# Two GpSimd steps and a later sum in the first pass of a retention stage

## The chip, the cores and the metric

The kernel runs on one core of one Trainium2 chip. The metric is the device time of one execution in microseconds (us), less is better. A measurement is a set of executions; the median is compared.

## What is computed

The kernel runs a two-layer backbone over 256 context tokens and 1024 latent tokens of width 1024. In each layer one combined projection feeds four mixers (a short convolution, latent attention, RWKV-7 and retention); their outputs are joined and projected, and a mixture of 16 experts follows. The change lies in retention alone, whose start is:

```python
def rotate(t, cos, sin):
    t1, t2 = jnp.split(t, 2, axis=-1)
    return jnp.concatenate([t1 * cos - t2 * sin, t1 * sin + t2 * cos], axis=-1)

def ret_project(z, rot):
    q, k, v, g = jnp.split(z.astype(jnp.float32), 4, axis=-1)
    q = split_heads(q, RET_HEADS) * (RET_DK ** -0.5)
    k = split_heads(k, RET_HEADS)
    if rot is not None:
        q = rotate(q, *rot)
        k = rotate(k, *rot)
    return q, k, split_heads(v, RET_HEADS), g

# per chunk of 128 tokens, for each of 4 heads (64 wide), forward and on flipped tokens:
    zeta = jnp.exp((RET_CHUNK - 1 - j)[:, None] * log_gamma[None, :])
    d_r = jnp.einsum('bnchk,bnchv->bnhkv', kc * zeta[None, None, :, :, None], vc)
    r_state * dec_c + dr_i
```

Context tokens are not rotated (`rot` is None), latent tokens are.

## The kernel before

Each layer runs as a row of stages. Each stage is one or more blocks, in which every engine has its own list of instructions and waits on semaphores; all engines meet at the end of a block. `stage_retention` has two blocks. The first one, here called the first pass, walks over the 10 tiles of 128 tokens (tiles 0 and 1 are context, 2 to 9 latent) in order. The change touches only this pass, once in each layer.

What each engine's list holds for tile t in the first pass, with the lines of the profile:

- **SyncE** (`rows_in`, L1353 and L1355) loads the tile's projected row `z` (128x1024, 512 KB) and, for latent tiles, the table `rope` (64 KB) into one of two slots. From tile 2 on it waits until the sum of tile t-2 is written and V of tile t-2 is copied.
- **VectorE** (`rotated`) makes the 8 heads of queries and keys, `qk`: for a context tile one copy (L1390); for a latent tile the direct product `ra` = z times cosine (L1393, 128x512), the crossed product `rb` = the other half of z times sine (L1396, two instructions of 8 runs of 32 columns), and their sum (L1398). Then `scaled_queries` (L1406, `QX`, two instructions) and `forward_state` (L1413, `SF`, two instructions, reading the forward sums from PSUM).
- **TensorE** (`turned`, L1471) transposes the tile's `qk` in four instructions; `sums` (L1484) makes keys times values of the tile before, 16 small products (8 of each direction) from `kz` and `V`.
- **ScalarE** computes the gate and copies V (`gate_values`, L1431 and L1432; here G and V), weighs the keys for the two directions (`weighed_keys`, L1450, 8 instructions of 128x64), copies the transposes out of PSUM (`turned_out`, L1436, `QT`) and copies the backward sums (`backward_sum`, L1440).
- **GpSimd** has nothing in this block. It makes the backward states (L1599, L1601) in the second one.

The order in these lists is written out by hand. VectorE's loop was: the rotation of tile t+1, then `QX` of tile t, then `SF` of tile t-1. ScalarE's loop: G and V of tile t+1, `kz` of t, `QT` of t, backward sum of t-1. TensorE's: transposes of t, sums of t-1.

The buffers that join the engines are `z`, `rope`, `qk` and `kz`, two slots each, and `ra` and `rb`, one each.

## Time and profile before

| what | us |
|---|---|
| median of 3 executions | 4108.26 |
| lowest, highest | 4102.06, 4124.47 |
| the profiled execution's own time | 4104.09 |
| span of its trace | 4102.3 |
| the first pass in layer 0, from 720.4 to 762.7 | 42.3 |
| the first pass in layer 1, from 2848.3 to 2890.2 | 41.9 |

Over the whole span TensorE is busy for 89%, VectorE for 54%, ScalarE for 26% and GpSimd for 12%. The shares are averages over stages that differ: the two first passes together are 84.2 us, 2.1% of the span, and have to be read by themselves, from the timeline. In them a row of the timeline gives the start, the length, the engine, the line, the tile written and the tiles read, how many instructions are merged in the row, and in brackets how long the engine was idle before it and who released it. Merged instructions overlap a little, so two of 0.42 can show as 0.76.

### The profile page before, as it was taken

To read this page: it belongs to the slowest core of one execution; us is meant where nothing else is said; L and a number is where in the kernel's file an instruction comes from. 1 tells how busy PE (TensorE), PEld (TensorE's weight loads), DVE (VectorE), ACT (ScalarE), POOL (GpSimd) and SP (SyncE) were. 2 spreads that over 40 slices of the span, in tenths; PEclk is the share of its full clock that TensorE was granted. 3 is DMA by queue.
4 is the path that set the end of the run, shared out by engine and by line. 5 is a ranking of instruction groups with operands and counts; after the bars stand their busy time and mean duration, and the time that the engine had idled before them with its cause. 6 is when DMAs were issued, how large, how long until landed. Compare 5 with 4: busy or idle time off the path is not lost. (4 is left out here: it accounts for less than half of the span.)

```text
span 4102.3 us, 65871 instructions
## 1 busy us (share of the span) xinstructions
PE 3640.6 (89%) x27258; PEld 2016.9 (49%) x27258; DVE 2226.3 (54%) x3698; ACT 1063.0 (26%) x2366; POOL 490.1 (12%) x675
## 2 busy tenths in 40 slices
PE   7899999687896699999997899998697876999998
PEld 4555665476633233333333655674586532333333
DVE  2554324687745644444443554335778667655654
ACT  3442110634311111111111542112544211212121
POOL 1100000231201011111111200000232110010100
PEclk9999999698998799999998999998698987999999
DMA  6200120200275587777774100121100336999996
GB/s 252 104 1 11 58 76 0 90 4 19 74 259 219 209 272 262 261 261 261 261 254 138 34 6 11 59 70 47 43 10 13 120 130 237 341 320 332 326 323 209
DMA packets 293591, 613.12 MB, mean 149 GB/s; under 512 B 37640, under 2 KB 50184, under 8 KB 286640
## 3 DMA queue, kind: packets, MB, share of 16 engines
q1 hardware_dynamic: 272752, 542.32, 37.2%
q0 software_dynamic: 20544, 66.60, 6.3%
q8 instruction: 219, 3.59, 0.4%
q14 instruction: 76, 0.62, 0.0%
HBM read 561.07 MB, written 47.79 MB: 148 GB/s over the span
## 5 line engine op out<-in xcount | busy, mean ns | idle before, releaser
L2991 PE MATMUL ps<-moe_w,e_hT 128*128 128x512 f32 x1024 | 449.4, 597 | 21.2 <-issue 9.2
L3120 DVE TENSOR_TENSOR moe_w<-moe_w 128x2048 f32<-128x2048 f32 x128 | 287.2, 2286 | 206.1 <-PE ps L2922 160.5
L2892 PE MATMUL ps<-moe_w,e_xs 128*64 128x512 f32 x1536 | 348.6, 596 | 0.8 <-DVE moe_w L3120 0.8
L2892 PE MATMUL ps<-moe_w,e_xT 128*64 128x512 f32 x1536 | 345.8, 600 | 0.8 <-DVE moe_w L3120 0.8
L2991 PEld LDWEIGHTS ps<-moe_w,e_hT 128*128 128x128 f32 x1024 | 192.3, 190 | 258.1 <-issue 255.3
L3126 DVE TENSOR_TENSOR e_cb<-e_part,ps 128x512 f32<-128x512 f32 x128 | 87.8, 686 | 335.1 <-ACT e_part L3028 249.2
L2892 PEld LDWEIGHTS ps<-moe_w,e_xT 128*64 128x64 f32 x1536 | 111.9, 139 | 222.9 <-issue 222.8
L2892 PEld LDWEIGHTS ps<-moe_w,e_xs 128*64 128x64 f32 x1536 | 105.4, 137 | 193.7 <-issue 192.3
L1184 PE MATMUL ps<-M 96*128 96x512 f32 (+1 forms) x400 | 182.4, 542 | 3.7 <-PEq L749 2.1
L3028 ACT COPY e_part<-ps 128x512 f32<-128x512 f32 x96 | 56.2, 585 | 487.4 <-PE ps L2892 479.1
L478 ACT COPY yT<-ps 128x256 f32<-128x256 f32 (+1 forms) x90 | 42.4, 471 | 402.8 <-PE ps L390 402.8
L1048 PE MATMUL ps<-yT,hT 128*128 128x272 f32 (+1 forms) x608 | 145.5, 393 | 0.0
L3120 DVE TENSOR_TENSOR moe_w<-e_t,moe_w 128x2048 f32<-128x2048 f32 x64 | 143.5, 2284 | 0.0
L1196 PEld LDWEIGHTS ps<-all_tabs,a_pr 128*128 128x128 f32 x656 | 74.6, 142 | 129.8 <-issue 88.3
L3120 DVE TENSOR_TENSOR e_t<-moe_w 128x2048 f32<-128x2048 f32 x60 | 134.6, 2284 | 0.0
L1245 DVE COPY a_pt<-ps 128x512 f32<-128x512 f32 (+1 forms) x104 | 61.2, 589 | 129.1 <-PE ps L1196 128.5
L1196 PE MATMUL ps<-all_tabs,a_pr 128*128 128x128 f32 x656 | 111.9, 284 | 20.4 <-ACT a_pt L1245 13.8
L2854 POOL DMA_INDIRECT x_rows<-e_ye,all_tok x16 | 52.7, 3291 | 639.4 <-DVE e_ye L3161 639.4
L1260 DVE TENSOR_REDUCE a_mx<-ps 128x1 f32<-128x1280 f32 (+1 forms) x72 | 98.5, 1368 | 52.0 <-PE ps L1184 52.0
L1048 PEld LDWEIGHTS ps<-yT,hT 128*128 128x128 f32 x608 | 113.6, 195 | 21.5 <-issue 1.3
L2854 POOL DMA_INDIRECT out_dram<-e_ye,all_tok x16 | 52.2, 3263 | 598.5 <-DVE e_ye L3161 598.5
L1287 ACT ACTIVATE a_pr<-ps,a_mx 128x1280 f32<-128x1280 f32 (+1 forms) x72 | 88.7, 1232 | 112.7 <-DVE a_mx L1261 112.7
(417 smaller groups left out, 7075.4 us busy)
## 6 DMA issues: line engine op xcount, KB each, us to landing
moe_w<-in_w_gate_dram SPq DMA_DIRECT2D x128, 1024.0 KB, 13.7
moe_w<-in_w_up_dram SPq DMA_DIRECT2D x128, 1024.0 KB, 14.2
moe_w<-in_w_down_dram SPq DMA_DIRECT2D x128, 1024.0 KB, 12.9
m_mod_w<-in_w_ada_dram SPq DMA_DIRECT2D x24, 1024.0 KB, 6.6
o_mod_w<-in_w_ada_dram SPq DMA_DIRECT2D x24, 1024.0 KB, 7.6
yT<-in_w_in_dram SPq DMA_DIRECT2D x6, 2048.0 KB, 8.6
r_z<-z_rows SPq DMA_DIRECT2D x20, 512.0 KB, 3.3
z_rows<-p_zo POOLq DMA_DIRECT2D x36, 256.0 KB, 2.3
```

The costliest lines, as they stand in the source:

```text
L1048: ins = nc.tensor.matmul(ps[:, ZBANK[a], 0:hi - lo], hT[:, k, t * P:(t + 1) * P], w[:, k, lo:hi], start=(k == 0), stop=(k == KT - 1))
L1184: ins = nc.tensor.matmul(ps[:, SB[u % 2] + i, 0:w], QT[0:QK, h, t * P:(t + 1) * P], KTr[0:QK, h, n:n + w], start=True, stop=True)
L1196: ins = nc.tensor.transpose(ps[:, TB, k * P:(k + 1) * P], pr[:, u % NP, (k0 + k) * P:(k0 + k + 1) * P], g.ident)
L1245: copy(pt[:, k % 2, u % 2, k0:k0 + nk].rearrange("p k n -> p (k n)"), ps[:, TB, 0:nk * P]).then_inc(*done.up())
L1260: link(nc.vector.reduce_max(mx[:, s % 2, 0:1], src, AX_X))
L1287: nc.scalar.activation(pr[:, s % NP, 0:units[s][2] * P], src, ACT.Exp, bias=mx[:, s % 2, 1:2], scale=SCALE, accum_out=rs[:, s // 2 % 4, s ...
L2854: pool.indirect_dma_start(dst, bass.IndirectOffsetOnAxis(ap=g.tok[:, 0, e:e + 1], axis=0), ye[:], None, compute_op=ALU.add).then_inc(*sc.u ...
L2892: ins = nc.tensor.matmul(ps[HF * q:HF * q + HF, b, :], x[:, k], weights[q][:, k], start=(first and k == 0), stop=(k == 3), skip_group_chec ...
L2991: ins = nc.tensor.matmul(ps[:, YB + c, :], hT2[:, 4 * half + k], quarter(name, e)[:, k], start=(half == 0 and k == 0), stop=(half == 1 and ...
L3028: nc.scalar.copy(part[:, i], ps[:, A_]).then_inc(*tcd.up())
L3120: nc.vector.tensor_tensor(to, a, b, ALU.subtract).then_inc(*td.up())
L3126: nc.vector.tensor_tensor(out_of(c), part[:, 1 if c == C12 else 0], ps[:, b], ALU.subtract if c == C21 else ALU.add).then_inc(*cd.up())
```

## The change

1. VectorE no longer makes the crossed product. GpSimd does, with the same two instructions of 8 runs of 32 columns (`crossed_part`), for latent tiles.
2. The keys weighed for the backward direction, four ScalarE instructions of 128x64 before, become one GpSimd instruction of 128x256 (`weighed_backward`). ScalarE keeps the four of the forward direction.
3. The rotation is split: the direct product of tile t+1 (`direct_part`) stays at the head of VectorE's loop, the sum (`rotated`) moves behind `QX` of tile t and `SF` of tile t-1.
4. New semaphores: `rad` (direct product), `rbd` (crossed product), `kzb` (backward keys). VectorE's sum waits for all three, TensorE's `sums` for `kzb`.

```diff
--- before.py
+++ after.py
@@ -1343,6 +1343,7 @@
         z_in, small, chain = [sg(f"w_slot{i}") for i in range(2)], sg("small_in"), sg("dve_chain")
         qkd, tr, ev_a, vd = sg("normed"), sg("transposed"), sg("evac_a"), sg("rt_zd")
         kzd, rm, fw, bw, wiped = sg("rt_kz"), sg("rt_rm"), sg("rt_rev"), sg("rt_bw"), sg("coef")
+        rad, rbd, kzb = sg("rt_ra"), sg("rt_rb"), sg("rt_kzb")
         with nc.Block() as block:
             @block.sync
             def _(sp):
@@ -1373,28 +1374,31 @@
                     n += 16 if u < NCT else 32
                 return n
 
+            def z8(t):
+                return z[:, t % 2, 0:512].rearrange("p (h d) -> p h d", h=8)
+
             @block.vector
             def _(dve):
                 link = linker(dve, chain)
 
+                def direct_part(t):
+                    dve.wait_ge(*z_in[t % 2].at(z_at(t)))
+                    if t >= NCT:
+                        if t > NCT:
+                            dve.wait_ge(*qkd.at(t))
+                        nc.vector.tensor_tensor(ra[:], z8(t), rope[:, t % 2, 0].unsqueeze(1).broadcast_to([P, 8, HD]), ALU.mult).then_inc(*rad.up())
+
                 def rotated(t):
-                    zz, q = z[:, t % 2], qk[:, t % 2]
-                    dve.wait_ge(*z_in[t % 2].at(z_at(t)))
-                    z8 = zz[:, 0:512].rearrange("p (h d) -> p h d", h=8)
-                    if t >= 1:
-                        dve.wait_ge(*qkd.at(t))
+                    q = qk[:, t % 2]
                     if t >= 2:
                         dve.wait_ge(*tr.at(t - 1))
                         dve.wait_ge(*kzd.at(t - 1))
+                        dve.wait_ge(*kzb.at(t - 1))
                     if t < NCT:
-                        nc.vector.tensor_copy(q, z8).then_inc(*qkd.up())
+                        nc.vector.tensor_copy(q, z8(t)).then_inc(*qkd.up())
                     else:
-                        r = rope[:, t % 2]
-                        link(nc.vector.tensor_tensor(ra[:], z8, r[:, 0].unsqueeze(1).broadcast_to([P, 8, HD]), ALU.mult))
-                        for s in range(2):
-                            a, b = 32 * s, 32 * (1 - s)
-                            link(nc.vector.tensor_tensor(rb[:, :, a:a + 32], z8[:, :, b:b + 32],
-                                                         r[:, 1, a:a + 32].unsqueeze(1).broadcast_to([P, 8, 32]), ALU.mult))
+                        dve.wait_ge(*rad.at(t - NCT + 1))
+                        dve.wait_ge(*rbd.at(t - NCT + 1))
                         nc.vector.tensor_tensor(q, ra[:], rb[:], ALU.add).then_inc(*qkd.up())
 
                 def scaled_queries(t):
@@ -1416,13 +1420,43 @@
 
                 link(nc.vector.memset(SF[:, 0], 0.0))
                 nc.vector.memset(ps[:, 2:6], 0.0).then_inc(*wiped.up())
+                direct_part(0)
                 rotated(0)
                 for t in range(NT):
                     if t + 1 < NT:
-                        rotated(t + 1)
+                        direct_part(t + 1)
+                    if t == 0:
+                        rotated(1)
                     scaled_queries(t)
                     if t >= 1:
                         forward_state(t - 1)
+                    if 1 <= t < NT - 1:
+                        rotated(t + 1)
+
+            @block.gpsimd
+            def _(pool):
+                def crossed_part(t):
+                    pool.wait_ge(*z_in[t % 2].at(z_at(t)))
+                    if t > NCT:
+                        pool.wait_ge(*qkd.at(t))
+                    for i in range(2):
+                        a, b = 32 * i, 32 * (1 - i)
+                        ins = nc.gpsimd.tensor_tensor(rb[:, :, a:a + 32], z8(t)[:, :, b:b + 32],
+                                                      rope[:, t % 2, 1, a:a + 32].unsqueeze(1).broadcast_to([P, 8, 32]), ALU.mult)
+                    ins.then_inc(*rbd.up())
+
+                def weighed_backward(t):
+                    if t == 0:
+                        pool.wait_ge(*small.at(80))
+                    pool.wait_ge(*qkd.at(t + 1))
+                    if t >= 2:
+                        pool.wait_ge(*rm.at(t - 1))
+                    nc.gpsimd.tensor_tensor(kz[:, t % 2, 1], qk[:, t % 2, 4:8].rearrange("p h d -> p (h d)"), ze[:, 1], ALU.mult).then_inc(*kzb.up())
+
+                for t in range(NT):
+                    if NCT <= t + 1 < NT:
+                        crossed_part(t + 1)
+                    weighed_backward(t)
 
             @block.scalar
             def _(act):
@@ -1445,10 +1479,9 @@
                     act.wait_ge(*qkd.at(t + 1))
                     if t >= 2:
                         act.wait_ge(*rm.at(t - 1))
-                    for d in range(2):
-                        for h in range(H):
-                            ins = nc.scalar.activation(kz[:, t % 2, d, h * HD:(h + 1) * HD], qk[:, t % 2, 4 + h], ACT.Copy,
-                                                       scale=ze[:, d, h * HD:h * HD + 1])
+                    for h in range(H):
+                        ins = nc.scalar.activation(kz[:, t % 2, 0, h * HD:(h + 1) * HD], qk[:, t % 2, 4 + h], ACT.Copy,
+                                                   scale=ze[:, 0, h * HD:h * HD + 1])
                     ins.then_inc(*kzd.up())
 
                 gate_values(0)
@@ -1474,6 +1507,7 @@
 
                 def sums(t):
                     pe.wait_ge(*kzd.at(t + 1))
+                    pe.wait_ge(*kzb.at(t + 1))
                     pe.wait_ge(*vd.at(t + 1))
                     if t >= 2:
                         pe.wait_ge(*fw.at(t - 1))
```

VectorE before, first pass of layer 0, from the rotation of tile 2 on. The rows give line, operation, tile written, tiles read and shape; x2 means two in a row:

```order
L1393 TENSOR_TENSOR r_ra<-r_z,r_rope 128x512
L1396 TENSOR_TENSOR r_rb<-r_z,r_rope 128x8x32 x2
L1398 TENSOR_TENSOR r_qk<-r_ra,r_rb 128x512
L1406 TENSOR_TENSOR r_QX<-r_QT,r_xi 128x2x128 x2
L1413 SCALAR_TENSOR_TENSOR r_SF<-r_SF,r_gd,ps 128x128 x2
```

VectorE in the changed kernel, the same place:

```order
L1389 TENSOR_TENSOR r_ra<-r_z,r_rope 128x512
L1410 TENSOR_TENSOR r_QX<-r_QT,r_xi 128x2x128 x2
L1417 SCALAR_TENSOR_TENSOR r_SF<-r_SF,r_gd,ps 128x128 x2
L1402 TENSOR_TENSOR r_qk<-r_ra,r_rb 128x512
L1389 TENSOR_TENSOR r_ra<-r_z,r_rope 128x512
```

The crossed product is gone from the list, and the sum (L1398 before, L1402 now) stands behind `QX` and `SF`.

GpSimd in the changed kernel, first pass of layer 0, from its start; before there was no row of this engine here:

```order
L1454 TENSOR_TENSOR r_kz<-r_qk,r_ze 128x256
L1444 TENSOR_TENSOR r_rb<-r_z,r_rope 128x8x32 x2
L1454 TENSOR_TENSOR r_kz<-r_qk,r_ze 128x256
L1444 TENSOR_TENSOR r_rb<-r_z,r_rope 128x8x32 x2
L1454 TENSOR_TENSOR r_kz<-r_qk,r_ze 128x256
```

The crossed product of tile t+1 stands ahead of the backward keys of tile t, all the way to the end of the pass.

## Rows read from the trace of the kernel before

**Rows 1.** The page's first line: span and number of instructions.

```profile
span 4102.3 us, 65871 instructions
```

**Rows 2.** Stretches: length; busy PE, PEld, DVE, ACT, POOL; clock; DMA share; GB/s.

```profile
720.40:762.70 42.30, 21.67 (x200) 16.51 (x200) 31.88 (x74) 34.90 (x121) 0.00 (x0) 0.50 0.47 156
...
733.55:758.63 25.08, 15.17 (x140) 11.55 (x140) 23.62 (x58) 23.49 (x86) 0.00 (x0) 0.50 0.45 142
2861.54:2886.13 24.59, 15.20 (x140) 11.58 (x140) 23.51 (x58) 23.47 (x85) 0.00 (x0) 0.50 0.45 145
```

**Rows 3.** Timeline, layer 0: the sum of tile 2 to the sum of tile 5.

```profile
732.86 0.69 DVE L1398 TENSOR_TENSOR r_qk<-r_ra,r_rb 128x512 f32<-128x512 f32 x1
...
733.58 0.33 SPq L1353 DMA_DIRECT2D r_z<-z_rows  x1
...
733.61 1.12 PE L1471 MATMUL ps<-all_tabs,r_qk 128*128 128x128 f32 x4 [2.46 <-DVE r_qk L1398]
...
738.08 0.42 ACT L1431 ACTIVATE r_G<-r_z 128x256 f32<-128x256 f32 x1 [0.96 <-DMA r_rope<-const_rope_r_dram]
...
738.24 1.12 PE L1484 MATMUL ps<-r_V,r_kz 128*64 128x64 f32 x16
...
738.70 2.02 ACT L1450 ACTIVATE r_kz<-r_qk,r_ze 128x64 f32<-128x64 f32 x8
...
740.62 0.56 ACT L1436 COPY r_QT<-ps 128x512 f32<-128x512 f32 x1
...
741.22 0.76 DVE L1406 TENSOR_TENSOR r_QX<-r_QT,r_xi 128x256 f32<-128x256 f32 x2 [0.64 <-ACT r_QT L1436]
...
741.89 0.60 DVE L1413 SCALAR_TENSOR_TENSOR r_SF<-r_SF,r_gd,ps 128x128 f32<-128x128 f32 x2
...
742.41 0.69 DVE L1393 TENSOR_TENSOR r_ra<-r_z,r_rope 128x512 f32<-128x512 f32 x1
743.13 0.88 DVE L1396 TENSOR_TENSOR r_rb<-r_z,r_rope 128x256 f32<-128x256 f32 x2
...
744.05 0.69 DVE L1398 TENSOR_TENSOR r_qk<-r_ra,r_rb 128x512 f32<-128x512 f32 x1
```

**Rows 4.** Timeline, layer 0: load of tile 7 issued, and its first reader.

```profile
744.77 0.33 SPq L1353 DMA_DIRECT2D r_z<-z_rows  x1
...
748.43 0.42 ACT L1431 ACTIVATE r_G<-r_z 128x256 f32<-128x256 f32 x1 [0.44 <-DMA r_rope<-const_rope_r_dram]
```

**Rows 5.** Timeline, layer 1: load of tile 4 issued, and its first reader.

```profile
2861.57 0.33 SPq L1353 DMA_DIRECT2D r_z<-z_rows  x1
...
2865.65 0.42 ACT L1431 ACTIVATE r_G<-r_z 128x256 f32<-128x256 f32 x1 [0.67 <-DMA r_rope<-const_rope_r_dram]
```

**Rows 6.** Timeline, layer 0: first keys weighed, and the end of the pass.

```profile
727.96 2.02 ACT L1450 ACTIVATE r_kz<-r_qk,r_ze 128x64 f32<-128x64 f32 x8 [1.91 <-DMA r_gr<-in_g_ret_norm_dram]
...
757.94 0.69 DVE L1398 TENSOR_TENSOR r_qk<-r_ra,r_rb 128x512 f32<-128x512 f32 x1
...
761.86 0.60 DVE L1413 SCALAR_TENSOR_TENSOR r_SF<-r_SF,r_gd,ps 128x128 f32<-128x128 f32 x2
761.90 0.37 ACT L1440 COPY yT<-ps 128x256 f32<-128x256 f32 x1 [0.48 <-PE ps L1484]
```

**Rows 7.** GpSimd and VectorE lines of the second block: ns min/median/max, first and last start.

```profile
L1599 POOL TENSOR_TENSOR r_SB<-r_SB,r_gd x18: 602/612/614, 763.1 to 2909.1; 128x256 f32<-128x256 f32 x18
...
L1601 POOL TENSOR_TENSOR r_SB<-r_SB,yT x18: 717/834/843, 763.8 to 2909.7; 128x256 f32<-128x256 f32 x18
...
L1578 DVE TENSOR_TENSOR r_on<-r_on,r_G x18: 424/424/427, 770.8 to 2920.4; 128x256 f32<-128x256 f32 x18
```

**Rows 8.** Timeline, second block: GpSimd beside a VectorE instruction with two SBUF inputs.

```profile
770.83 0.42 DVE L1578 TENSOR_TENSOR r_on<-r_on,r_G 128x256 f32<-128x256 f32 x1
771.00 0.84 POOL L1601 TENSOR_TENSOR r_SB<-r_SB,yT 128x256 f32<-128x256 f32 x1
```

## Prediction

> **What bounds the kernel now.** I read the timeline of the two first passes, since the page's shares say nothing about 2% of a span of 4102.3 us [rows 1]. Let S(t) be the end of the sum of tile t. Seven periods lie between S(2) = 732.86 + 0.69 = 733.55 and S(9) = 757.94 + 0.69 = 758.63 [rows 3, 6]: 25.08 us in layer 0, and 24.59 in layer 1, so 3.58 and 3.51 us a tile. VectorE is busy for 23.62 of the 25.08 and ScalarE for 23.49, GpSimd for nothing [rows 2]. The reader should see two nearly full engines and conclude, first, that taking work from both ought to help; and then look at what fills a period. VectorE's list goes `ra`, `rb`, sum, `QX`, `SF`, by starts 742.41, 743.13, 744.05 and 741.22, 741.89 [rows 3]: from `QX` to `SF` 0.67, from `SF` to `ra` 0.52, `ra` 0.72, `rb` 0.92, sum 0.69, together about 3.5. This order has a property that no busy share shows. Behind S(t) VectorE had 2.3 us of rotation of the next tile to do while TensorE transposed and ScalarE copied out, so `QX` seldom waited.
>
> A second chain runs through the loads. `z` and `rope` have two slots, so tile t+2 is asked for at S(t): 733.58 for tile 4, behind S(2) = 733.55. ScalarE's G of tile 4 starts at 738.08, released by the `rope` load [rows 3]. I call this L = time from S(t) to G of tile t+2: 4.53 there, 4.11 for the same tile in layer 1 (2865.65 less 2861.54) [rows 2, 5], 3.69 for tile 7 (748.43 less the end of the sum at 744.05 + 0.69 = 744.74) [rows 3, 4]. G stands ahead of `kz` and `QT` of the tile before in ScalarE's list. So S(5) = S(2) + L 4.53 + G and V 0.62 + eight `kz` 1.92 + `QT` to `QX` 0.60 + 0.67 + 0.52 + the rotation 2.33 = 744.74, which is just the 744.05 + 0.69 of the trace [rows 3]. Before, this chain spanned three tiles, 11.19 at worst, and bit once a layer.
>
> **The change part by part.** *Crossed product off VectorE.* Two instructions, 0.92 us of a period [rows 3], are taken from VectorE. *Backward keys off ScalarE.* Four of eight instructions at 1.92 / 8 = 0.24 each by starts: 0.96 [rows 3]. As engine work this leaves VectorE 2.6 and ScalarE about 2.3 us a tile. *The sum moved last.* Here the gain goes. The sum of tile t+1 now stands behind `QX` of tile t, which waits for `QT` of t, which waits for the transposes of t, which wait for S(t). Of the rotation only `ra` (0.69) still lies under that latency. From S(t) on: 0.06 to the first transpose (733.61 less 733.55), 1.12 for the four, 0.04 to ScalarE, so `QT` starts at +1.22; the four `kz` of about 0.05 + 0.96 = +1.01 are just hidden beside them. Then `QT` start to `QX` start 0.60, `QX` to `SF` 0.67, `SF` to what follows 0.52, sum 0.69 [rows 3]. That is **3.70 us** from S(t) to S(t+1), against 3.58 and 3.51 before. TensorE's 16 products of `sums` follow the transposes by 1.04 or so and take 1.12 [rows 3], ending at +2.3, ahead of `SF` at +2.49: hidden.
>
> *GpSimd's side.* Its three instructions are released at S(t) too. The trace has no product of 8 runs of 32 columns on this engine. The nearest rows are its 128x256 products and sums, 0.61 and 0.72 to 0.84 [rows 7]; a short run could be up to twice as dear. A pair at 0.61 to 0.84 takes 1.2 to 1.7; even if it starts only behind `ra`, at +0.72, it is there by +1.9 to +2.4, and the sum starts at +3.01. It is covered, and stays so up to 1.14 us an instruction. The backward keys, one more of 0.6 to 0.84, end by +3.3 and are asked for by `sums` in the next period, at about +1.1 there: covered.
>
> *The two engines at once.* With both on the same SBUF tiles they may hold each other up. Where `r_on<-r_on,r_G` of VectorE (both inputs in SBUF) overlapped GpSimd's L1601, GpSimd took 0.84 in place of 0.72, while VectorE kept its 424 ns, at most 427 over 18 [rows 7, 8]. No row that I read shows a VectorE instruction of this kind that starts in the middle of a GpSimd one. The bounds are 0 and a full block of `QX` until GpSimd is done (the rival below, 1.1 us a tile); I take c = 0.15 a tile, near the row, since `QX` at +1.82 meets at most the end of the second crossed instruction. The period is 3.85.
>
> *The loads' chain gets shorter in tiles.* Now S(t+2) = S(t) + L + 0.62 + 0.96 + 0.60 + 0.67 + 0.52 + 0.69 = S(t) + L + 4.06 + c: it spans two tiles where it spanned three. With L = 3.69 that is 7.90 for two tiles, 3.95 each, a little over 3.85; with the slow first loads it is 8.74 in layer 0 and 8.32 in layer 1. Nothing hides this.
>
> *Start and end of the pass.* `kz` of tile 0 starts at 727.96 when the constants have landed [rows 6]. Then `QT` +0.96, G and V of tile 2 +0.60, `kz` of 1 +0.62, `QT` +0.96, `QX` +0.60, `SF` +0.67, sum +0.52, its end +0.69: S(2) = 733.58, as before (733.55): what the four `kz` give is paid for by the sum's place. Behind S(9) the last copy ended at 761.90 + 0.37 = 762.27, 3.64 later, and `SF` at 762.46, 3.83 later [rows 6]. Now the sums of tile 9 end at about +3.2 and their copy at +3.6, and `SF` at +3.1: 0.2 gained.
>
> *The sum.* With these rules, layer 0: S(2) 733.7, S(3) 737.6, S(4) 742.5 (loads), S(5) 746.3, S(6) 750.4, S(7) 754.2, S(8) 758.3, S(9) 762.1, against 758.63: +3.5. Layer 1: +3.6. Less 0.2 each: +6.7 us in all. Engines meet at the block's end, so the shift passes to the end of the kernel whole, and nothing behind it changes. Against the profiled execution's own time, 4104.09 + 6.7 = 4110.8; I say **4111**. That execution lay 4.2 below the median of its three (4108.26), so a median might well read 4115. With c = 0 it is +5.2.
>
> **The rivals.**
>
> *A, the engines' work decides (faster).* If `QT` came much sooner than I reckon, the period would be VectorE's 2.6, held by the loads to at least (3.69 + 4.06) / 2 = 3.88 unless G's wait too were gone. At 2.6 a tile, seven periods give 18.2, about 6.6 less a layer, 4091. Against it: the trace shows every link of the 3.70, and none is GpSimd's or `rb`.
>
> *B, the loads are quick (no difference).* If L falls to 3.3 or less, the period is 3.70 all through: 25.9 a layer, +0.8 and +1.3, less 0.4: 4106. For it: L varies from 4.53 to 3.69. Against: each L measured is over 3.6.
>
> *C, the engines shut each other out (slower).* `QX`'s two instructions start at +1.82, when GpSimd is in its run of three. If GpSimd, once it has begun, is let through to its end (0.72 + 3 times 0.73 = +2.9), `QX` comes 1.1 late in each period: 4.8 a tile, S(9) at 768.4 in layer 0, +9.7 and +10.1, less 0.4, 4123.5; if VectorE slips in ahead of the backward keys, c = 0.8 and 4119. It decides from the point where GpSimd still holds the tiles at +1.82, that is, once a crossed instruction takes over 0.55 us behind `ra`. For it: the 0.12 that GpSimd lost beside VectorE [rows 8]. Against: VectorE itself has lost nothing in 18 instances [rows 7]. The Trainium skill, "SBUF — State Buffer", section "Who interferes with whom", says that a VectorE instruction with two SBUF inputs contends with a GpSimd instruction that reads SBUF, and that whoever starts first gets the shared pair for the whole instruction. By that rule `ra`, `QX` and the sum all contend, and the outcome is this rival's 4119 to 4123.5 in place of 4111; the 0.12 us of the row agrees with its half in which GpSimd is the loser.
>
> **How the numbers follow.** Forecast (c from 0 to 0.3: 4109 to 4112.5) 0.60; C (4117 to 4124) 0.20; B 0.10; A 0.06; something in GpSimd that is dearer than twice its rows, beyond 4124, 0.04. Eight in ten, with the few us by which medians of this kernel stand from the profiled execution, need 4100 to 4123. About 0.5%, 20 us, is what a measurement of this kernel can tell from no change (its three times spread over 22). Nearly all cases lie inside: faster by more 0.03, within 0.92, slower by more 0.05.
>
> **What would show it.** In the changed trace: `QX` idle in each period, released by `QT`; the time from transposes to `QT` start to `QX` to `SF` to sum of 3.7 to 3.85; in every other period ScalarE's G released by `rope` with `kz` right behind it; VectorE's busy time down by about 6 of 23.6 us in this stretch and its idle time up by more; `rb` on GpSimd done before `SF` starts. C is told by `QX` starting well after `QT`'s end, or by `QX` or GpSimd rows longer than 0.42 and 0.84. I am wrong if the sum waits for GpSimd, if the gap S(2) to S(9) shrinks below 25, or if the time moves outside the two first passes.

## The result, and the profile after

The changed kernel takes 4124.11 us (median of 20 executions, 4109.93 to 4137.73) against 4109.41 us before (median of 20, 4098.97 to 4124.47): the ratio is 1.004, with a 95% interval from 1.0029 to 1.0051. It is slower by 14.7 us, inside the half per cent called no change ahead of the result. The forecast was 4111 with a range from 4100 to 4123, so it missed, its upper end by 1.1 us. The profiled execution of the changed kernel took 4124.27 us.

The page's first line and the stretches of the changed kernel, as [rows 1, 2] show them of before. The columns of a stretch are its length, then busy PE, PEld, DVE, ACT and POOL, then the clock, the DMA share and GB/s; DVE is VectorE, ACT ScalarE, POOL GpSimd, PE TensorE, PEld its weight loads, and further down SPq the queue of SyncE. The first two stretches are the first passes of layers 0 and 1, the third runs from S(2) to S(9) of layer 0, where S(t) is the end of the sum of tile t as in the prediction:

```profile
span 4122.1 us, 65855 instructions
...
720.22:769.98 49.76, 21.52 (x200) 16.42 (x200) 29.88 (x58) 27.70 (x81) 23.36 (x27) 0.50 0.40 133
2847.61:2897.21 49.60, 21.53 (x200) 16.44 (x200) 29.86 (x58) 27.29 (x81) 23.34 (x27) 0.50 0.41 133
735.18:766.22 31.04, 15.17 (x140) 11.55 (x140) 22.07 (x43) 18.04 (x54) 19.31 (x21) 0.50 0.35 115
```

Two things are to be seen. The passes are 49.8 and 49.6 us long. And VectorE is still busy for 22.07 us between S(2) and S(9), where it was for 23.62 [rows 2]: 14 crossed instructions are gone from that stretch, with 0.88 x 7 = 6.2 us of busy time [rows 3], but the busy time fell by only 1.55. What is left of its list has grown by some 4.6 us.

To compare kernels I take a pass from the first issue of a `z` load to GpSimd's first memset of the second block. By that measure both passes together are 84.16 us before (42.27 and 41.89) and 99.36 after (49.76 and 49.60), so 15.2 us more, against 14.7 in the medians. Where they sit:

| part of the pass | layer 0 before, after | layer 1 before, after | difference | forecast |
|---|---|---|---|---|
| first load issued to S(2) | 13.07, 14.96 | 13.19, 14.48 | +1.89, +1.29 | about 0 |
| seven periods, S(2) to S(9) | 25.08, 31.04 | 24.59, 31.36 | +5.96, +6.77 | +3.5, +3.6 |
| S(9) to the end | 4.12, 3.76 | 4.11, 3.76 | -0.36, -0.35 | -0.2, -0.2 |
| sum | | | +15.2 | +6.7 |

One period of the changed kernel, timeline of layer 0 from S(2) = 735.18 to S(3) = 739.51. The columns are start, length, engine, line, operation, tile written and tiles read, number of merged instructions, and the idle time before with its releaser:

```profile
735.24 1.11 PE L1504 MATMUL ps<-all_tabs,r_qk 128*128 128x128 f32 x4 [5.00 <-DVE r_qk L1402]
...
735.28 0.69 DVE L1389 TENSOR_TENSOR r_ra<-r_z,r_rope 128x512 f32<-128x512 f32 x1
735.33 1.93 POOL L1444 TENSOR_TENSOR r_rb<-r_z,r_rope 128x256 f32<-128x256 f32 x2 [1.88 <-DVE r_qk L1402]
...
736.39 0.59 ACT L1470 COPY r_QT<-ps 128x512 f32<-128x512 f32 x1
737.00 1.39 DVE L1410 TENSOR_TENSOR r_QX<-r_QT,r_xi 128x256 f32<-128x256 f32 x2 [1.03 <-ACT r_QT L1470]
737.21 0.91 POOL L1454 TENSOR_TENSOR r_kz<-r_qk,r_ze 128x256 f32<-128x256 f32 x1
...
738.32 0.59 DVE L1417 SCALAR_TENSOR_TENSOR r_SF<-r_SF,r_gd,ps 128x128 f32<-128x128 f32 x2
...
738.83 0.68 DVE L1402 TENSOR_TENSOR r_qk<-r_ra,r_rb 128x512 f32<-128x512 f32 x1
```

The first half is the forecast's, to within 0.01 us: `QT` starts at S + 1.21 (forecast 1.22), `QX` at S + 1.82 (forecast 1.82), and `QX` has waited 1.03 us for `QT`. From there on it is not. `QX` takes 1.39 us where it took 0.76 [rows 3], and `SF` starts 1.32 behind it, not 0.67. The period is 1.21 + 0.61 + 1.32 + 0.51 + 0.68 = 4.33 us, and 4.32 to 4.33 in six of the seven of each layer.

The same lines over both passes, ns min/median/max of one instruction, then first and last start:

```profile
L1410 DVE TENSOR_TENSOR r_QX<-r_QT,r_xi x40: 412/521/943, 729.6 to 2895.6; 128x256 f32<-128x256 f32 x40
...
L1444 POOL TENSOR_TENSOR r_rb<-r_z,r_rope x32: 716/978/1240, 730.9 to 2890.5; 128x256 f32<-128x256 f32 x32
...
L1454 POOL TENSOR_TENSOR r_kz<-r_qk,r_ze x20: 720/900/913, 728.0 to 2893.5; 128x256 f32<-128x256 f32 x20
```

A `QX` instruction took 418 to 427 ns before. Now half of them take over 521, up to 943. GpSimd's instructions take 716 and 720 at best and up to 1240. The trace even holds its own control, at the end of layer 0's pass, where there is no further tile to rotate and GpSimd makes the backward keys alone, well ahead of `QX`:

```profile
766.29 0.73 POOL L1454 TENSOR_TENSOR r_kz<-r_qk,r_ze 128x256 f32<-128x256 f32 x1 [1.48 <-DVE r_qk L1402]
...
768.04 0.76 DVE L1410 TENSOR_TENSOR r_QX<-r_QT,r_xi 128x256 f32<-128x256 f32 x2 [1.82 <-ACT r_QT L1470]
```

Both engines are back to 0.73 and 0.76. It looks like the third rival, the engines shutting each other out. Whether it is that, and how much of the loss it makes, the experiments tell.

### The profile page after: what moved, and what is told of

Same layout as the page of the kernel before. It is cut to its first block and busy times, and to the rows that moved or that the text cites. A ratio compares the mean times of both kernels' runs of the same rounds, so it can differ in the third digit from the quotient of the medians.

```text
span 4122.1 us, 65855 instructions
## 1 busy us (share of the span) xinstructions
PE 3640.0 (88%) x27258; PEld 2018.0 (49%) x27258; DVE 2222.4 (54%) x3666; ACT 1049.2 (25%) x2286; POOL 537.6 (13%) x727
## 6 DMA issues: line engine op xcount, KB each, us to landing
moe_w<-in_w_gate_dram SPq DMA_DIRECT2D x128, 1024.0 KB, 14.1
```

## The experiments

The theories. **Contention**: the 0.63 us a tile is VectorE and GpSimd holding each other up when both read SBUF. **Order**: whatever the contention, the sum's place costs by itself. **Loads**: the passes are held up by the two slots. The table gives what each run showed; a pass is measured as above, periods are S to S, and a time is a median where there are several executions, with its ratio to the kernel before as it was measured beside that run.

| run | both passes, us | typical period | time, us |
|---|---|---|---|
| before | 84.16 | 3.43 to 3.47 | 4109.41 (20) |
| after | 99.36 | 4.33 | 4124.11 (20), 1.004 |
| e1_write_only | 91.08 | 3.69 to 3.72 in six of 14, others to 4.24, one 4.82 | 4110.73 (1) |
| e2_no_backward | 92.67 | 3.80 to 4.01, one 5.55 | 4115.14 (1) |
| e3_cross_vector | 92.99 | 3.81 to 4.12, three 4.56 to 5.43 | 4116.09 (1) |
| e4_sum_first | 86.58 | 3.46 and 3.62, one 4.92 | 4107.63 (10), 1.0003 |
| e5_third_slot | 99.28 | 4.33 | 4122.07 (1) |
| e6_queries_psum | 85.24 | 3.48 | 4112.13 (1) |
| e7_all_three | 78.19 | 3.03 | 4100.34 (12), 0.9974 |
| e8_before_third_slot | 86.99 | 3.43 | 4110.06 (10), 0.9998 |
| e9_order_alone | 104.77 | 4.50 | 4132.06 (1) |
| e10_first_psum | 84.34 | 3.24 and 3.64 | 4114.83 (1) |
| e11_all_three_late | 77.07 | 3.03 | 4102.94 (12), 0.9988 |

A single time says little here. The span less the two passes, which no edit touches, lies between 4015.6 and 4029.4 us in these traces: 14 us of spread that belong to none of the changes. What follows is read from the passes, and times decide only where there are ten or more. The passes have a spread of their own: from the first load issued to the first keys, which wait for the small constants, it is 7.3 to 7.9 us in most traces with two slots, but 9.21 and 8.13 in e4_sum_first, 8.27 and 8.78 in e9_order_alone and 8.10 in layer 0 of e10_first_psum, though SyncE's list is the same in all of them. The periods don't contain this part and are the surer measure.

### GpSimd writes only

```diff
-                        nc.vector.tensor_tensor(q, ra[:], rb[:], ALU.add).then_inc(*qkd.up())
+                        nc.vector.tensor_tensor(q, ra[:], ra[:], ALU.add).then_inc(*qkd.up())
...
-                    for i in range(2):
-                        a, b = 32 * i, 32 * (1 - i)
-                        ins = nc.gpsimd.tensor_tensor(rb[:, :, a:a + 32], z8(t)[:, :, b:b + 32], ..., ALU.mult)
-                    ins.then_inc(*rbd.up())
+                    scratch = SB[:].rearrange("p t a n -> p (t a n)")
...
+                    nc.gpsimd.memset(scratch[:, 0:1856], 0.0).then_inc(*rbd.up())
...
+                        nc.gpsimd.memset(SB[:].rearrange("p t a n -> p (t a n)")[:, 1856:2560], 0.0).then_inc(*kzb.up())
```

> The changed kernel, but GpSimd only writes: its two crossed products are one memset of 1856 columns of an unused buffer (estimated 1.7 us from the 1.38 us of its 1536-column memset in the trace of before), and its backward keys of tiles 2 to 9 a memset of 704 columns (0.7 us); the sum on VectorE adds the direct product to itself. That leaves out the crossed half of the rotation and the backward keys. GpSimd stays busy for as long as before, at the same places. Theory 1 (VectorE's instructions with two SBUF inputs and GpSimd's reads shut each other out): QX's two take 0.76 us again in place of 1.39, and the period of a tile is 1.21 + 0.61 + 0.67 + 0.51 + 0.68 = 3.7 us, up to 3.9 where the loads hold it, in place of 4.33. Theory 2 (any work of GpSimd beside VectorE slows it, writes too): QX stays at 1.2 us or more and the period at 4.2 or more.

The same period in layer 0, timeline, and the line of `QX` over both passes:

```profile
735.15 1.65 POOL L1445 MEMSET r_SB<- 128x1856 f32 x1 [1.84 <-DVE r_qk L1402]
...
736.73 0.68 POOL L1457 MEMSET r_SB<- 128x704 f32 x1
...
736.87 0.76 DVE L1410 TENSOR_TENSOR r_QX<-r_QT,r_xi 128x256 f32<-128x256 f32 x2 [1.03 <-ACT r_QT L1473]
...
L1410 DVE TENSOR_TENSOR r_QX<-r_QT,r_xi x40: 411/422/460, 729.9 to 2892.0; 128x256 f32<-128x256 f32 x40
```

GpSimd is busy beside all of `QX` but its last 0.22 us (to 737.41 of 737.63), and `QX` takes its 0.76. The period is 3.70 where no load is late: the forecast's sum with c = 0, c being its term for what the two engines take from each other. So it is not GpSimd's being busy, nor its writing to SBUF, that stretches `QX`; it is its reading. The Trainium skill, "SBUF — State Buffer", section "Who interferes with whom", says that a VectorE instruction with two SBUF inputs contends with a GpSimd instruction that reads SBUF and not with one that only writes it; these rows agree on the half about writing, and the `QX` of 1.39 in the changed kernel on the half about reading.

### No backward keys on GpSimd

```diff
-                    nc.gpsimd.tensor_tensor(kz[:, t % 2, 1], qk[:, t % 2, 4:8].rearrange("p h d -> p (h d)"), ze[:, 1], ALU.mult).then_inc(*kzb.up())
+                    if t < 2:
+                        nc.gpsimd.tensor_tensor(kz[:, t % 2, 1], qk[:, t % 2, 4:8].rearrange("p h d -> p (h d)"), ze[:, 1], ALU.mult).then_inc(*kzb.up())
+                    else:
...
+                        nc.gpsimd.memset(SB[:, 0, 0, 0:1], 0.0).then_inc(*kzb.up())
```

> The changed kernel, but GpSimd's backward keys of tiles 2 to 9 are left out (a memset of one column signals in their place). Theory 1: QX's first instruction keeps its 0.53 us (it meets the end of the crossed product), the second falls from 0.94 to 0.42, since nothing reads beside it; the period falls by 0.52 to 3.8 us, 3.9 where the loads hold it. Theory 2, or if the second crossed instruction alone is the obstacle: the period stays over 4.2.

`QX` in layer 0, timeline: the pair, and in an answer that starts later its first instruction alone:

```profile
737.70 0.86 DVE L1410 TENSOR_TENSOR r_QX<-r_QT,r_xi 128x256 f32<-128x256 f32 x2 [1.03 <-ACT r_QT L1474]
```
```profile
737.70 0.53 DVE L1410 TENSOR_TENSOR r_QX<-r_QT,r_xi 128x256 f32<-128x256 f32 x1 [1.03 <-ACT r_QT L1474]
```

The first instruction still takes 0.53 (it meets the end of the crossed product, as in the changed kernel), the second is free, and the period is 3.81 where no load is late. That splits the 0.63 of the changed kernel: 0.11 come from the crossed product, 0.52 from the backward keys, which start between the two `QX` instructions and shut the second one out.

### The crossed product back on VectorE

```diff
                         nc.vector.tensor_tensor(ra[:], z8(t), rope[:, t % 2, 0].unsqueeze(1).broadcast_to([P, 8, HD]), ALU.mult).then_inc(*rad.up())
+                        for i in range(2):
+                            a, b = 32 * i, 32 * (1 - i)
+                            ins = nc.vector.tensor_tensor(rb[:, :, a:a + 32], z8(t)[:, :, b:b + 32], ..., ALU.mult)
+                        ins.then_inc(*rbd.up())
...
                 for t in range(NT):
-                    if NCT <= t + 1 < NT:
-                        crossed_part(t + 1)
                     weighed_backward(t)
```

> The changed kernel with the crossed product back on VectorE, behind the direct one; the sum stays last and the backward keys stay on GpSimd. This is the order with one GpSimd instruction a tile, which runs beside the products. Theory 1, with the sum's place costing by itself: the products take 1.6 us and up to 0.6 more beside GpSimd's read, so QX starts at 1.82 to 2.2 behind the sum, QX's two take 0.76, and the period is 3.7 to 4.1 us, above the 3.5 to 3.6 of before although GpSimd no longer meets QX. Rival (the sum's place costs nothing, all the loss is contention): 3.5 or less.

Timeline, layer 0:

```profile
734.76 0.74 DVE L1415 TENSOR_TENSOR r_QX<-r_QT,r_xi 128x256 f32<-128x256 f32 x2
...
736.70 0.73 POOL L1459 TENSOR_TENSOR r_kz<-r_qk,r_ze 128x256 f32<-128x256 f32 x1 [3.09 <-DVE r_qk L1407]
...
736.73 1.25 DVE L1389 TENSOR_TENSOR r_ra<-r_z,r_rope 128x512 f32<-128x512 f32 x1
...
738.61 0.76 DVE L1415 TENSOR_TENSOR r_QX<-r_QT,r_xi 128x256 f32<-128x256 f32 x2
```

This shows that either engine can be the one that loses. GpSimd starts 0.03 us ahead and keeps its 0.73; VectorE's `ra` takes 1.25 in place of 0.69, just until GpSimd is done (737.43) and 0.55 more. In the changed kernel `ra` was ahead by 0.05 (735.28, 735.33) and it was GpSimd's first crossed instruction that took 1.24. In these rows whoever begins first keeps its time. And with most of the contention gone from the chain the period is 3.82, still longer than the 3.43 to 3.47 of before. At most 0.13 of that is the stretched `ra`: `QX` of tile 2 starts at S(2) + 1.95 (734.76 less 732.81), where it was + 1.82 in the changed kernel; the rest, over 0.2 us a tile, is not contention.

### The old order, without GpSimd

The kernel before, with only the sum moved behind `QX` and `SF`:

```diff
-                    if t >= 2:
-                        dve.wait_ge(*tr.at(t - 1))
-                        dve.wait_ge(*kzd.at(t - 1))
...
-                        nc.vector.tensor_tensor(q, ra[:], rb[:], ALU.add).then_inc(*qkd.up())
+
+                def summed(t):
+                    if t >= NCT:
+                        dve.wait_ge(*tr.at(t - 1))
+                        dve.wait_ge(*kzd.at(t - 1))
+                        nc.vector.tensor_tensor(qk[:, t % 2], ra[:], rb[:], ALU.add).then_inc(*qkd.up())
...
                         forward_state(t - 1)
+                    if t + 1 < NT:
+                        summed(t + 1)
```

> The kernel before with nothing but the sum moved behind QX and SF; VectorE still makes both products and ScalarE all eight key instructions; GpSimd has no work in the pass, so nothing can contend. Theory (the place of the sum costs the latency through TensorE and ScalarE): behind S(t) the eight key instructions take 0.05 + 1.92 and only then comes QT, so the period is 1.97 + 0.60 + 0.67 + 0.52 + 0.69 = 4.45 us in place of 3.43: the passes get about 14 us longer in all. Rival (the order is harmless by itself): 3.6 or less.

Timeline, layer 0, from S(3) = 739.44:

```profile
739.47 2.02 ACT L1454 ACTIVATE r_kz<-r_qk,r_ze 128x64 f32<-128x64 f32 x8 [1.14 <-DVE r_qk L1400]
...
741.39 0.56 ACT L1440 COPY r_QT<-ps 128x512 f32<-128x512 f32 x1
...
742.06 0.76 DVE L1408 TENSOR_TENSOR r_QX<-r_QT,r_xi 128x256 f32<-128x256 f32 x2 [0.91 <-ACT r_QT L1440]
...
743.25 0.68 DVE L1400 TENSOR_TENSOR r_qk<-r_ra,r_rb 128x512 f32<-128x512 f32 x1
```

No GpSimd, no contention (`QX` 0.76), and the slowest kernel of all: 4.50 a period, both passes 20.6 us longer than before, where about 14 were expected. The seven periods of each layer give 14.8 of it, about as expected; the other 5.8 lie at the start, 1.9 a layer by the new order and 2.0 in all because the constants landed later in this trace. With the sum last, all eight `kz` stand on the chain ahead of `QT`. Moving half of them, and the crossed product, to GpSimd takes the period to 4.33 and the passes from 104.77 to 99.36, 5.4 us less, of which 1.6 are again only the constants. So the order is what makes the changed kernel slower, and the two moves to GpSimd pay back about a fifth of what it costs.

### The new work, with the sum first

```diff
                         direct_part(t + 1)
-                    if t == 0:
-                        rotated(1)
+                        rotated(t + 1)
                     scaled_queries(t)
...
                         forward_state(t - 1)
-                    if 1 <= t < NT - 1:
-                        rotated(t + 1)
```

> The changed kernel with the sum back at its old place, ahead of QX and SF; GpSimd keeps both of its steps. Theory 1: the latency through TensorE and ScalarE is hidden again, so the period is VectorE's work, 0.67 + 0.52 + 0.72 + 0.69 = 2.6 us, and what the two engines take from each other, 0.5 to 1.0, so 3.1 to 3.6 us a tile against 4.33 and against 3.5 of before: 4099 to 4110 us beside a before of 4109. Rival (the order is not to blame, GpSimd's steps are): 4 us a tile or more, 4117 or more.

Timeline, layer 0, and the line of the sum over both passes:

```profile
749.60 2.02 POOL L1441 TENSOR_TENSOR r_rb<-r_z,r_rope 128x256 f32<-128x256 f32 x2 [0.91 <-DMA r_rope<-const_rope_r_dram]
...
751.76 1.10 DVE L1402 TENSOR_TENSOR r_qk<-r_ra,r_rb 128x512 f32<-128x512 f32 x1 [0.71 <-POOL r_rb L1441]
...
752.78 1.28 DVE L1410 TENSOR_TENSOR r_QX<-r_QT,r_xi 128x256 f32<-128x256 f32 x2
...
L1402 DVE TENSOR_TENSOR r_qk<-r_ra,r_rb x16: 691/998/1103, 733.1 to 2886.2; 128x512 f32<-128x512 f32 x16
```

Putting the order back takes 12.8 of the 15.2 us back: 86.58 against 99.36. But the gain of the GpSimd work over the old kernel does not appear (84.16). Of the 2.4 us above it, 1.8 lie before S(2), where the constants came later than before by 1.73 and 0.53; the periods are no shorter either (50.9 in all, 49.7 before). Now the sum waits in every second tile for the crossed product (0.71), whose `rope` landed late, and is itself stretched from 0.69 to a median of 1.00, since the backward keys begin just ahead of it; and `QX` still takes 1.28 in some tiles, beside the crossed product. In time the kernel is the same as before, 1.0003 with an interval from 0.9987 to 1.0019.

### QX from PSUM

`QX` reads the transposes where TensorE left them, and ScalarE's copy of them waits for `QX`. The order stays the changed kernel's.

```diff
-                    dve.wait_ge(*ev_a.at(t + 1))
+                    dve.wait_ge(*tr.at(t + 1))
...
-                        nc.vector.tensor_tensor(QX[:, :, d, ts], QT[:, 0:2, ts], xi[:, :, d], ALU.mult)
+                        ins = nc.vector.tensor_tensor(QX[:, :, d, ts], ps[:, t % 2, 0:2 * P].rearrange("p (a n) -> p a n", a=2), xi[:, :, d], ALU.mult)
+                    ins.then_inc(*qxd.up())
...
-                    act.wait_ge(*tr.at(t + 1))
+                    act.wait_ge(*qxd.at(t + 1))
...
+                        pe.wait_ge(*qxd.at(t - 1))
```

> The changed kernel, but VectorE makes QX straight from the transposes in PSUM, ahead of ScalarE's copy of them, which now waits for QX (one PSUM bank, one engine at a time). Theory: QX starts 1.21 us behind the sum in place of 1.82, and as it has one SBUF input it meets nothing of GpSimd, so its two take 0.76 in place of 1.39. SF then waits for TensorE's sums, at about +2.3, and the sum starts at +2.8: a period of about 3.5 us in place of 4.33, a little more where the loads hold it. If the contention did not come from the second SBUF input, QX would stay at 1.2 us or more: 3.9 or more.

The line of `QX` over both passes, and `SF` in layer 0:

```profile
L1410 DVE TENSOR_TENSOR r_QX<-ps,r_xi x40: 414/417/425, 732.4 to 2889.9; 128x256 f32<-128x256 f32 x40
```
```profile
740.73 0.60 DVE L1418 SCALAR_TENSOR_TENSOR r_SF<-r_SF,r_gd,ps 128x128 f32<-128x128 f32 x2 [0.31 <-PE ps L1520]
```

Of 40 `QX` instructions none is over 425 ns, with GpSimd's list as it was. Having one input in PSUM ends the contention for `QX`; it also takes ScalarE's copy out of the chain. Now `SF` waits for the sums of TensorE, the period is 3.48 and the passes are 14.1 us shorter than the changed kernel's, though the sum still stands last. `QX` from PSUM and the sum first together (e10_first_psum) give little more:

> The version with all three parts less two of them: two load slots again, and the direct product in SBUF, so that the sum has two SBUF inputs. Sum ahead of QX, QX from PSUM, GpSimd's two steps stay. Theory: the sum meets the backward keys and is stretched to 0.9 to 1.1 us (0.69 with nothing beside it), so a period is 3.2 to 3.3 where the loads let it, and every second tile waits for rope as with the sum first alone: 3.3 to 3.6 in the mean, against 3.03 with all three. If the third slot and the PSUM product are worth nothing: 3.03.

Periods of 3.24 and 3.64 in turn, 84.34 us: with the sum first what is left is the sum, which waits 0.72 us for the crossed product in every second tile, where `rope` lands late, and is stretched to 0.90 to 1.10 beside the backward keys.

### The loads

In most passes of the kernels with two slots one period is longer than its neighbours by 0.4 to 1.8 us, because one load comes late. In the changed kernel's layer 0 it is tile 5's. It is issued at S(3), and its first reader starts 5.01 us behind S(3) = 739.51; the load of tile 4 took 738.82 less 735.18, or 3.64:

```profile
738.82 0.42 ACT L1465 ACTIVATE r_G<-r_z 128x256 f32<-128x256 f32 x1 [0.99 <-DMA r_rope<-const_rope_r_dram]
...
739.54 0.33 SPq L1354 DMA_DIRECT2D r_z<-z_rows  x1
...
744.52 0.42 ACT L1465 ACTIVATE r_G<-r_z 128x256 f32<-128x256 f32 x1 [2.37 <-DMA r_rope<-const_rope_r_dram]
```

It makes one period 5.07 there (5.41 in layer 1). A third slot was to hide it, in the changed kernel and in the one before; the third `z` and `rope` lie in a part of `yT` that this pass doesn't use:

```diff
+        zs = [z_[:, 0], z_[:, 1], yT[:, 6, 0:W_RET]]
+        ropes = [rope_[:, 0], rope_[:, 1], yT[:, 7, 0:2 * HD].rearrange("p (c f) -> p c f", c=2)]
...
-                    if t >= 2:
-                        sp.wait_ge(*qkd.at(t - 1))
-                        sp.wait_ge(*vd.at(t - 1))
+                    if t >= 3:
+                        sp.wait_ge(*qkd.at(t - 2))
+                        sp.wait_ge(*vd.at(t - 2))
...
                 rows_in(1)
+                rows_in(2)
```

> The changed kernel with a third slot for z and rope (in a part of yT that is free in this pass), so that tile t+2's load no longer waits for the sum of tile t, and tile 2's load is issued at the very start. Theory: in the changed kernel the loads cost 1.6 us at the start (the sum of tile 2 is late because rope lands late) and 0.74 us once more (one period of 5.07 in place of 4.33 in layer 0); the rest of a period, 4.33, has nothing to do with them. So all seven periods become 4.33 and the pass gets 1.5 to 2.5 us shorter than its 49.8 us in layer 0. Rival (the loads set the common period too, by a second chain): the periods drop below 4.2.

> The kernel before with the third load slot alone. Theory: its period is VectorE's 3.43 us and loads bite once a layer (4.17 in layer 0, 3.88 in layer 1), so seven periods drop from 25.08 and 24.59 to about 24.1 each: 1.4 us in all, not to be told from no change in the time (4105 to 4108 beside 4107). This is the control for what of the version with all three comes from the slot.

Both expectations on the passes were wrong, in the same way. The late load is hidden: all 14 periods are 4.32 to 4.34 in the one, 3.43 to 3.45 in the other. But nothing is gained, 99.28 against 99.36 and 86.99 against 84.16, because tile 2's load now stands ahead of the small constants in SyncE's list. ScalarE's first keys wait for them, in e8_before_third_slot for 4.50 us where it was 1.91 [rows 6]. Counted from the first issue, these keys come there 2.95 and 1.44 us later than before, and S(2) 2.95 and 1.45:

```profile
735.80 1.30 ACT L1453 ACTIVATE r_kz<-r_qk,r_ze 128x64 f32<-128x64 f32 x5 [4.50 <-DMA r_gr<-in_g_ret_norm_dram]
```

What the loads cost in the changed kernel is thus 0.73 us in layer 0 and 1.05 in layer 1 (31.04 and 31.36 less 7 x 4.33 = 30.31), not the main part. Why that one load takes 5 us and its neighbours 3.6 stays open.

### All together

The sum first, `QX` from PSUM, a third slot, and `ra` written to PSUM, so that the sum too has one input there:

```diff
-        ra = sb("ra", [P, 8, HD])
+        ra = ps[:, 6].rearrange("p (h d) -> p h d", h=8)
```

> GpSimd keeps its two steps, the sum is back ahead of QX, QX is made from PSUM, the direct product is written to a free PSUM bank (so that the sum too has only one SBUF input), and there is a third load slot. Only the direct product still has two SBUF inputs. Theory: nothing of GpSimd but the start of its first crossed instruction is held up, the period is VectorE's 2.6 us or GpSimd's three instructions, 2.2 plus up to 0.5, so 2.7 to 3.0 us a tile against 3.5 of before; the two passes get 8 to 12 us shorter in all than before: 0.2 to 0.3% faster, about 4098 beside 4107. Rival (GpSimd's steps cannot pay off here whatever the order): no faster than before.

Timeline, layer 0, and the line of the sum over both passes:

```profile
739.75 0.75 DVE L1413 TENSOR_TENSOR r_QX<-ps,r_xi 128x256 f32<-128x256 f32 x2
...
740.42 0.60 DVE L1421 SCALAR_TENSOR_TENSOR r_SF<-r_SF,r_gd,ps 128x128 f32<-128x128 f32 x2
...
740.93 1.03 DVE L1392 TENSOR_TENSOR ps<-yT 128x512 f32<-128x512 f32 x1
...
741.35 1.18 POOL L1455 TENSOR_TENSOR r_kz<-r_qk,r_ze 128x256 f32<-128x256 f32 x1
...
742.19 0.69 DVE L1405 TENSOR_TENSOR r_qk<-ps,r_rb 128x512 f32<-128x512 f32 x1 [0.23 <-DVE ps L1392]
...
L1405 DVE TENSOR_TENSOR r_qk<-ps,r_rb x16: 691/692/692, 733.1 to 2877.6; 128x512 f32<-128x512 f32 x16
```

The period is 3.03 or 3.04 throughout, and VectorE is what fills it: from `QX` to `SF` 0.67, to `ra` 0.51, `ra` with its 0.23 of idle 1.26, the sum 0.60. The sum is back at 692 ns for all 16, `QX` at 416. Only `ra`, which still reads two tiles in SBUF, is stretched (1.03). The passes are 78.19 us, 6.0 shorter than before: the periods give 7.2 (25.08 and 24.59 less 21.23 and 21.25), start and end take 1.2 back, 0.97 of it to S(2) in layer 0 (14.04 against 13.07). The 8 to 12 that were expected counted on shorter periods and an unchanged start. The time is 4100.34 us, 0.9974 of the kernel before with an interval from 0.9963 to 0.9986: faster than both kernels, if by a quarter of a per cent. The ratio is about 11 us, more than the 6.0 of the passes, but its interval reaches down to that. The last run puts the third load behind the constants:

```diff
                 rows_in(1)
-                rows_in(2)
                 for name, dst in (("zeta", ze), ("xi", xi), ("gdec", gd), ("dmat", dm)):
...
-                for t in range(3, NT):
+                for t in range(2, NT):
                     rows_in(t)
```

> The version with all three parts, but the third slot's first load (tile 2) is issued behind the constants, as before, and not ahead of them. Theory: with the load ahead of the constants the first sum of a rotated tile ended 14.04 and 12.93 us after the pass began, 16.0 and 14.6 in the kernel before with a third slot, 13.1 and 13.2 without; the constants come later by about the transfer of the third row of tiles, about 1 us. Periods stay at 3.03; the two passes are 0 to 2 us shorter than 78.2 in all: about 4098, the same as the version with all three within what can be measured, and 0.2 to 0.4% faster than before.

S(2) comes 12.94 and 12.91 us behind the first issue (14.04 and 12.93 with the load ahead), as it should be if the place of that load cost the time in layer 0, and the passes are 77.07, 7.1 shorter than before. The time, 4102.94 and 0.9988 with an interval from 0.9976 to 1.0000, is less of a gain than the 0.2 to 0.4% expected, and doesn't tell it from e7_all_three, whose interval it overlaps: a gain of a microsecond is under what times resolve here.

## Why the prediction was wrong, by its steps

- **That the sum's place eats the gain: right.** `QT` at +1.21 and `QX` at +1.82 came as reckoned, `QX` idle for 1.03 us in each period, the order alone 4.50, and 3.70 with GpSimd reading nothing.
- **GpSimd's side: right in what it concluded.** The crossed pair of the period shown ended at 735.33 + 1.93 = 737.26, +2.08, inside the +1.9 to +2.4, and the sum never waited for it. Unstretched, 8 runs of 32 columns cost 716 ns, no more than a dense 128x256.
- **The two engines at once: the step that failed.** It took c = 0.15 a tile, since `QX` "meets at most the end of the second crossed instruction". That meeting did cost 0.11 (e2_no_backward). What the term left out is the second meeting: the backward keys, queued right behind, begin while the first `QX` instruction runs and hold the second one for 0.52. c was 0.63 in place of 0.15. Against 0.15 this is 0.48 x 14 = 6.7 us over the two layers; 5.6 of them appear in the result (5.96 + 6.77 less 7.1), since the forecast had spent some on waits for loads that the longer period hides. The evidence used for the small value, VectorE's 424 ns in [rows 7, 8], came from cases in which VectorE had begun first: in the row shown (770.83 against 771.00) and in all ten of the 18 that overlap a GpSimd product or sum, by 0.16 to 0.18 us each time; the other eight had none beside them. They say who loses when GpSimd comes second, and nothing on GpSimd first. The forecast's own sign shows the miss: VectorE's busy time was to fall by about 6 us between S(2) and S(9) and fell by 1.55.
- **Rival C was what happened**, in its milder form ("if VectorE slips in ahead of the backward keys, c = 0.8 and 4119"). 4104.09 + 15.2 is 4119.3 by the profiled execution's base, but that this meets the 4119 is luck: 3.2 of the 15.2 are the late start, which the rival did not have, and it put c at 0.8 where 0.63 was measured. It had a chance of 0.20 against 0.60 for a mechanism with the contention nearly absent. The rule of the Trainium skill named in it ("SBUF — State Buffer", section "Who interferes with whom") held in these runs, and I weighed it by a row that did not test it.
- **The start of the pass: wrong, "S(2) = 733.58, as before".** It came 1.89 and 1.29 us later, counted from the first issue. The chain counted on G of tile 2 being 0.96 us earlier, as much as was saved on `kz`, and did not ask when its load lands. Before, G started at 730.49, 0.61 behind `QT`, with no wait. The start of the changed kernel, layer 0:

```profile
728.97 0.56 ACT L1470 COPY r_QT<-ps 128x512 f32<-128x512 f32 x1
...
730.81 0.42 ACT L1465 ACTIVATE r_G<-r_z 128x256 f32<-128x256 f32 x1 [1.28 <-DMA r_rope<-const_rope_r_dram]
...
732.99 1.07 DVE L1410 TENSOR_TENSOR r_QX<-r_QT,r_xi 128x256 f32<-128x256 f32 x2 [1.49 <-ACT r_QT L1470]
...
734.50 0.68 DVE L1402 TENSOR_TENSOR r_qk<-r_ra,r_rb 128x512 f32<-128x512 f32 x1
```

  G was ready to start at 728.97 + 0.60 = 729.57 and got its load at 730.81: 1.24 late. `QX` of tile 1 was stretched by 0.33 (`SF` follows it by 1.00, not 0.67), and the constants came 0.30 later. 1.24 + 0.33 + 0.30 = 1.87 of the 1.89. In layer 1 the same three are 0.91, 0.33 and 0.03.
- **The loads' chain: the mechanism was there, with other loads.** Tile 4 took 3.64 where 4.53 had been carried over from before, and another tile took 5.0. At a period of 4.33 the ordinary loads are hidden, and only the late one shows. Where c is 0, in e1_write_only, the chain is seen as reckoned: two neighbouring periods of layer 1 add up to 7.81 to 7.94 us, for 7.75 + c.
- **The end of the pass** gave 0.36 and 0.35, not 0.2.
- **The base.** The sum was put on the profiled execution's 4104.09, while saying that medians may read 4.2 higher. The median of the larger set of executions is 4109.41, 5.3 above it. With the forecast's own +6.7 that gives 4116.1; the other 8.5 us are the terms above (periods 5.6, starts 3.2, ends -0.3), which makes 4124.6. With any one of these right, the periods (5.6), the starts (3.2) or the base (5.3), the time would have come inside the range; the step that was wrong in mechanism is c. The chance of 0.92 for within half a per cent held.

## What to carry to other kernels

An order that keeps an engine full can be better than one that leaves it less work: putting the sum behind a round trip over TensorE and ScalarE put that round trip into every tile, and cost more than both moves to GpSimd gave. Write down the chain from one tile to the next for the new order, before counting busy time. When VectorE (with both inputs there) and GpSimd are both to read SBUF, price every pair of instructions that can meet, in both orders, and take as evidence that an engine loses nothing only rows in which the other began first; giving one of VectorE's two inputs a home in PSUM removes the meeting. A step that is made to start earlier needs the landing time of its load looked up, even where it did not wait before.

## What the runs showed of the hardware

- VectorE's instructions with both inputs in SBUF and GpSimd's that read SBUF took turns here, by whole instructions: 0.69 became 1.25 for `ra` when GpSimd began 0.03 us earlier, 0.72 became 1.24 for GpSimd when VectorE began 0.05 earlier. The one held up needs a little less than its full time once the other is done, 0.55 of 0.69 for `ra`. Two engines with back-to-back lists then interleaved, one instruction each: `QX`, keys, `QX`, which made 1.39 of 0.76.
- GpSimd memsets did not do this to VectorE (`QX` median 422 ns, at most 460), nor did a reading GpSimd do it to a VectorE instruction with one input in PSUM (`QX` 414 to 425, sum 691 to 692).
- In 9 of the 18 passes with two slots one load, of tile 4 or 5, took 4.9 to 5.4 us from issue to reader, where most others from tile 4 on, of the same 512 KB and 64 KB, took 3.6 to 4.0. It stays unexplained.
- The untouched rest of the program varied by 14 us between single executions, as much as the whole effect of this change; a single time can't tell such variants apart, while medians of 12 to 20 executions told the changed kernel and e7_all_three from the one before, and the passes, read from the traces, show where the difference lies.
